# Mixture-of-experts stage of a two-block transformer: expert slots taken in pairs as 512-column products, token picking and spreading in split fp32r

## The reference, cut to what matters

```python
def swiglu(x, w_gu, w_down):
    g, u = jnp.split(x @ w_gu, 2, axis=-1)
    return (jax.nn.silu(g) * u) @ w_down

def moe_ffn(x, router, w_gu, w_down):
    xt = x.reshape(B * S, D)                     # 256 x 1024
    logits = (xt @ router).astype(jnp.float32)
    top_v, top_i = lax.top_k(logits, TOP_K)      # 2 of 8
    w = jax.nn.softmax(top_v, axis=-1)
    combine = jnp.einsum('tk,tke->te', w, jax.nn.one_hot(top_i, N_EXPERTS))
    y = jnp.zeros_like(xt)
    for e in range(N_EXPERTS):
        y = y + combine[:, e:e + 1] * swiglu(xt, w_gu[e], w_down[e])
    return y.reshape(B, S, D)
```

## Time and profile before

| | us |
|---|---|
| median of 3 runs | 2509.06 (2503.76 to 2511.31) |
| the profiled execution, whole | 2510.95 |
| its span, first to last instruction | 2509.0 |
| expert loop in it, 1452.72 to 2481.69 | 1029 |

### The profile page before, as it was taken

One profiled execution on the slowest core, in us unless ns is written; L12 is line 12 of the kernel. 1 busy time (PEld: TensorE's weight loads), 2 busy tenths in 40 slices (PEclk: granted clock), 3 DMA queues, 4 the chain that ended last, 5 costly groups with the idle time before them and its releaser, 6 DMA issues.

```text
span 2509.0 us, 43797 instructions
## 1 busy us (share of the span) xinstructions
PE 2419.1 (96%) x18302; PEld 2308.8 (92%) x18302; DVE 1887.7 (75%) x2272; ACT 1359.5 (54%) x1532; POOL 2.4 (0%) x8
## 2 busy tenths in 40 slices
PE   7799999999999999999998899999999999999998
PEld 6689999999999999899996799999999999999997
DVE  6666596888565969654566588888888888888886
ACT  4446333454444333433426367777676667676765
POOL 0000000000000000000000000000000000000000
PEclk9999999999999999999999999999999999999999
DMA  5124344532333455355331179988999999888995
GB/s 224 72 101 142 126 180 176 192 135 101 122 144 130 169 184 185 147 184 185 136 121 39 68 264 357 345 341 341 340 343 338 343 342 340 340 343 339 345 340 217
DMA packets 77279, 557.23 MB, mean 222 GB/s; under 512 B 8608, under 2 KB 8736, under 8 KB 10144
## 3 DMA queue, kind: packets, MB, share of 16 engines
q1 hardware_dynamic: 75888, 547.45, 58.7%
q10 hardware_dynamic: 1008, 6.49, 0.7%
q0 software_dynamic: 192, 0.52, 0.1%
HBM read 552.86 MB, written 1.05 MB: 221 GB/s over the span
## 4 chain that ended last, share of the span: by engine, by line
PE 90%; ACT 4%; DVE 4%; issue 2%; DMA 1%; SPq 0%; DVEq 0%; ACTq 0%
PE ps L890 13%; PE ps L892 13%; PE ps L891 13%; PE ps L1451 12%; PE ps L1453 12%; PE ps L1452 12%; PE ps L970 2%; PE ps L1001 2%; PE ps L1491 1%; PE ps L1445 1%; ACT whi L510 1%; PE ps L897 1%; PE ps L1248 1%; PE ps L1111 1%; PE ps L1079 1%
## 5 line engine op out<-in xcount | busy, mean ns | idle before, releaser
L1577 DVE TENSOR_TENSOR wlo<-raw,whi 128x2048 fp32r<-128x2048 f32 x519 | 1185.9, 2290 | 316.7 <-ACT whi L510 259.4
L510 ACT ACTIVATE whi<-raw 128x2048 fp32r<-128x2048 f32 x519 | 993.8, 1915 | 528.7 <-PE ps L892 375.1
L890 PE MATMUL ps<-hh,whi 128*128 128x256 f32 x2080 | 596.7, 287 | 9.6 <-DVE hl L1645 7.1
L891 PE MATMUL ps<-hl,whi 128*128 128x256 f32 x2080 | 591.7, 284 | 0.0
L892 PE MATMUL ps<-hh,wlo 128*128 128x256 f32 x2080 | 591.6, 284 | 0.0
L1451 PE MATMUL ps<-whi,hh 128*128 128x256 f32 x1792 | 523.3, 292 | 3.6 <-DVE work L2263 3.6
L1453 PE MATMUL ps<-wlo,hh 128*128 128x256 f32 x1792 | 507.9, 283 | 0.0
L1452 PE MATMUL ps<-whi,hl 128*128 128x256 f32 x1792 | 507.6, 283 | 0.0
L890 PEld LDWEIGHTS ps<-hh,whi 128*128 128x128 f32 x2080 | 402.7, 194 | 12.3 <-DVE hl L1645 8.5
L891 PEld LDWEIGHTS ps<-hl,whi 128*128 128x128 f32 x2080 | 402.7, 194 | 0.3
L892 PEld LDWEIGHTS ps<-hh,wlo 128*128 128x128 f32 x2080 | 402.4, 193 | 0.0
(11 more groups left out here) (332 smaller groups left out, 2771.0 us busy)
## 6 DMA issues: line engine op xcount, KB each, us to landing
raw<-stream SPq DMA_DIRECT2D x519, 1024.0 KB, 4.9
work<-w_in ACTq DMA_DIRECT2D x1, 2240.0 KB, 8.6
stage<-stage_consts ACTq DMA_DIRECT2D x4, 512.0 KB, 4.7
work<-mem_in ACTq DMA_DIRECT2D x2, 1024.0 KB, 4.9
x<-x_in SPq DMA_DIRECT2D x1, 1024.0 KB, 4.8
out<-x SPq DMA_DIRECT2D x4, 256.0 KB, 2.3
const<-consts SPq DMA_DIRECT2D x1, 548.5 KB, 5.8
work<-work POOLq DMA_DIRECT2D x4, 128.0 KB, 2.6
```

The lines of the kernel that those rows point to most:

```text
L510: nc.scalar.activation(whi[hi_at(g, odd)][:, :], raw[g % RAWS][:, :], ACT.Copy).then_inc(hi_ready, 1)
L890: mm(out_ap, hi_w, hi_x, start=start, stop=False, **kw)
L891: mm(out_ap, hi_w, lo_x, start=False, stop=False, **kw)
L1577: V.tensor_tensor(wlo[g % RAWS][:, :], raw[g % RAWS][:, :], whi[hi_at(g, odd)][:, :].bitcast(F32), ALU.subtract).then_inc(lo_ready[g % RAW ...
```

## The change

Only the expert stage changes.

1. **Gate/up slots in pairs.** SP no longer loads gate/up slots as they lie: it loads for an even slot of a pair the first half of the input blocks of both slots, for the odd one the second half. A piece that lies together in HBM is then 2 KB, not 8 KB, and a transfer has four for each partition. A pair thus accumulates in one whole PSUM bank over its two slots: per slot 4 x 3 matmuls of 512 columns. silu, multiply, turn and both keeps now come once for a pair, 256 columns wide (the turn is two 128-column ones). VectorE's and ScalarE's keeps of a pair now stand two pairs later, in even slots, behind the split of that slot; the turn stands behind the odd slot of the next pair.
2. **Gather** in two fp32r halves of the tokens (the 0/1 matrix is exact) for two experts at once, 256 columns, in two rounds (behind down slots 1 and 3 of an odd expert's second half) that use the same two banks; VectorE keeps each round (`keep_gathered`, behind its split of down slots 2 and 4).
3. **Spread** in fp32r: the 0/1 matrix unweighted, and the result, scaled by the slot's weight while it is kept, in a high part (ScalarE) and a low part (VectorE, `few_keep_y_lo`).
4. Before the loop: one more VectorE subtraction (2048 columns), no weighted matrices, two stretches of 14 matmuls on zeros; the turns of the 0/1 matrices move into expert 0's slots 2 and 6, with 16 one-column products.
5. The other branch (an expert with over 128 tokens) is rewritten to the new slot layout; it isn't run.

```diff
+            with sp.Fori(0, EXPERTS) as e:
+                for g in range(FIRST, FIRST + PER_EXPERT):
+                    sp.wait_ge(slot_used, e * PER_EXPERT + (g + 1 - RAWS))
+                    at, half = expert_slot(g)
...
+                        two = stream[bass.ds(e * PER_EXPERT + at, 2)].rearrange("two p (b h x) -> p b two h x", b=2, h=2)
+                        sp.dma_start(to[:, :].rearrange("p (b two x) -> p b two x", b=2, two=2), two[:, :, :, half]).then_inc(
...
 ScalarE, gate/up slots
+                        if s % 2:
+                            act.wait_ge(slot_used, e * PER_EXPERT + (gu.g + s + 1))
+                            act.wait_ge(few_tok, e * HALF + (q + 1))
+                            nc.scalar.activation(few_gate(q), ps[:, q % 2, 0:2 * P], ACT.Silu).then_inc(gate_act, 1)
-                        if s:
-                            few_keep_hi(e, j - 1)
                         split_hi(gu.g + s + DEPTH, e, e % 2)
+                        if s % 2 == 0 and s >= 4:
+                            few_keep_hi(e, q - 2)
...
 TensorE
+                for c in range(NB // 2):
+                    n = e % 2 * NB + s % 2 * 4 + c
+                    at = slice(n * P, (n + 1) * P)
+                    last = split_x(ps[:, bank, :].rearrange("p (m n) -> p m n", m=4), hh[:, at], hl[:, at], by_in(whi[hi_at(g, e % 2)], c),
+                                   by_in(wlo[g % RAWS], c), start=(s % 2 == 0 and c == 0), stop=(s % 2 == 1 and c == NB // 2 - 1))
...
+            def few_turn(e, q):
+                pe.wait_ge(few_tok, e * HALF + (q + 3))
+                pe.wait_ge(act_ready, e * HALF + (PHASES["moe_gu0"].a + q))
+                for n in range(2):
+                    last = turn(ps[:, 7, n * P:(n + 1) * P], few_tok_act(q)[:, n * P:(n + 1) * P])
...
+                        if s % 2 == 1 and q % (HALF // 2):
+                            few_turn(e, q - 1)
...
+                        if part == 1 and e % 2 and e < EXPERTS - 1 and s in (1, 3):
+                            if s == 1:
                                 pe.wait_ge(y_added, e * 2 + 1)
+                            else:
+                                pe.wait_ge(gather_kept, e + 2)
+                            few_gather((e + 1) // 2, s // 2, 5)
...
 VectorE
-                            if s:
-                                few_keep_lo(e, j - 1)
+                            q = part * (HALF // 2) + s // 2
+                            if s % 2:
+                                dve.wait_ge(gate_act, e * HALF + (PHASES["moe_gu0"].a + q + 1))
+                                V.tensor_tensor(few_tok_act(q), few_gate(q), ps[:, q % 2, 2 * P:4 * P], ALU.mult).then_inc(few_tok, 1)
                             split_lo(gu.g + s + DEPTH, e, e % 2)
+                            if s % 2 == 0 and s >= 4:
+                                few_keep_lo(e, q - 2)
+                            if part == 0 and s == 3 and e:
+                                few_keep_y_lo(e - 1)
                         for s in range(down.n):
                             split_lo(down.g + s + DEPTH, e, e % 2)
+                            if s in (0, 2):
+                                few_keep_lo(e, q - 1 + s // 2)
+                            if part == 0 and e and s in (3, 6):
+                                add_y(e - 1, s // 6)
+                            if part == 1 and e % 2 and e < EXPERTS - 1 and s in (2, 4):
+                                keep_gathered((e + 1) // 2, s // 4)
```

More of the change, by code:

```diff
@@ L147, in build @@
         mask_r = over("mask_r", "stage", 512, F32R)
+        few_r = over("few_r", "work", 12288, F32R)
         ident_r = over("ident_r", "const", P, F32R)
@@ L1430, in _ @@
             last.then_inc(x_turned, 1)
+            keep_warm(7, 14)
             pe.wait_ge(picked, 1)
@@ L1439, in _, with few_gather, few_give, few_slot_weights @@
             last.then_inc(counts_ps, 1)
-            def few_gather(e):
-                for c in range(NB):
+            keep_warm(7, 14)
+            def few_gather(pair, r, bank):
+                takes = few_r[:, FEW_TAKE + pair * 512:FEW_TAKE + (pair + 1) * 512].rearrange("p (e t n) -> p t e n", e=2, t=2)
+                for c in range(4):
+                    n = 4 * r + c
+                    to = ps[:, bank + c // 2, (c % 2) * 256:(c % 2 + 1) * 256].rearrange("p (e n) -> p e n", e=2)
+                    for part, tokens in enumerate((FEW_TOK_HI, FEW_TOK_LO)):
+                        for tt in range(2):
+                            last = mm(to, tokens[:, tt * 1024 + n * P:tt * 1024 + (n + 1) * P], takes[:, tt],
+                                      start=part == 0 and tt == 0, stop=part == 1 and tt == 1)
+                last.then_inc(gathered_ps, 1)
+            def few_give(half):
+                pe.wait_ge(places_built, 2)
+                for n in range(8):
+                    last = turn(ps[:, 5 + n // 4, (n % 4) * P:(n % 4 + 1) * P], few_take(4 * half + n // 2, n % 2).bitcast(F32))
+                last.then_inc(spread_ps, 1)
+            def few_slot_weights():
+                for e in range(EXPERTS):
                     for tt in range(2):
-                        take = bass.ds(e * 256 + (FEW_TAKE + tt * P), P)
-                        last = mm(ps[:, 5 + c // 4, (c % 4) * P:(c % 4 + 1) * P], FEW_TOK[:, tt * 1024 + c * P:tt * 1024 + (c + 1) * P],
-                                  work[:, take], start=(tt == 0), stop=(tt == 1))
-                last.then_inc(gathered_ps, 1)
+                        last = mm(ps[:, 2, e:e + 1], few_take(e, tt).bitcast(F32), small[:, 576 + tt * 8 + e:577 + tt * 8 + e],
+                                  start=e == 0 and tt == 0, stop=tt == 1, skip_group_check=True)
+                last.then_inc(slot_weights_ps, 1)
             def split_x(out_ap, hi_x, lo_x, hi_w, lo_w, start, stop, **kw):
@@ new lines, in keep_gathered @@
+                def keep_gathered(pair, r):
+                    dve.wait_ge(gathered_ps, 2 * pair + r + 1)
+                    kept = [keep_x_hi(r, odd, 5) for odd in range(2)]
+                    for odd in range(2):
+                        lo = keep_x_lo(r, odd, 5, kept[odd])
+                        if r:
+                            lo.then_inc(gathered, 1)
+                    V.memset(small[:, 639:640], 0.0).then_inc(gather_kept, 1)
+                V.memset(small[:, 638:639], 0.0).then_inc(few_tok, 2)
@@ new lines, in _ @@
+                for odd in range(2):
+                    if odd == 0:
+                        dve.wait_ge(gathered_ps, 1)
+                    first = keep_x_hi(0, odd, 5)
+                    if odd == 0:
+                        dve.wait_ge(gathered_ps, 2)
+                    second = keep_x_hi(1, odd, 3)
+                    keep_x_lo(0, odd, 5, first)
+                    keep_x_lo(1, odd, 3, second).then_inc(gathered, 1)
+                V.memset(small[:, 639:640], 0.0).then_inc(gather_kept, 2)
```

242 lines of the change are left out of this document (137 added, 105 removed).

## The result

The changed kernel takes **2810.97 us** (2802.43 to 2816.16, 4 runs) beside 2510.18 us before (2503.76 to 2512.97, 4 runs): ratio 1.1199, 95% interval 1.1159 to 1.1239. That is 301 us, 12.0% slower. The forecast was 2678, its range ended at 2740; 133 us are missing, and they are the subject of what follows. The profiled execution, from which all rows here come, took 2815.7 us, 4.7 above the median.

What follows compares the result with a forecast made beforehand. TensorE's own order, its instructions and its waits for VectorE, was taken to bound the loop. Experts of 145.6 to 156.9 us sum to 1201 against 1029, +172; 2509.1 + 172 - 3.4 = 2678 us, range 2650 to 2740.

Steps and rivals of the forecast that it cites:

- The waits: Expert loop: turns 1 to 6 of each half wait 2.16 us for VectorE's low keep, 96 times, 207 us.
- the 4.88: Microseconds from an even slot's end until VectorE's splits and keep are done and the turn can start; TensorE needs only 2.72.
- Rival (3): TensorE's clock falls in the turn waits: +70 us (2748) in a quarter of the pairs, +280 in all; chance 0.08.
- The rest of the ring: Loop: turn, even slot, ScalarE's split, VectorE's split, keep, next turn, repeating every 7.8 us for each waiting pair.
- rival 2: Weight loads in 2 KB pieces become the bound: +3 to +15 us at 336 GB/s, 2748 at 290; chance 0.07.
- The work: Pure TensorE work of an expert without a gather: 119.1 us, some 8 less than before; 512-column matmuls 0.227 apart.
- rival (4): Gate/up slots: four-piece 512-column operands run slower, +0.1 us a slot giving 2690; chance included in the forecast's 0.78.
- The start of expert 0: 16 turns and 16 one-column products in expert 0, at 0.12 and 0.04 us, 2.6 in all; expert 0 takes 145.6.
- The gather: Experts 1, 3, 5: second round waits 4.8 us, next expert's first slot some 1.7; with 4.0 of gathering 10.7 each.
- The ends: Outside the expert loop: it starts near 1449.3, 3.4 us earlier than before; behind the loop no change.
- Rival (1): The keep is not late, so no turn waits: loop 987 us, kernel 2464, faster than before; chance 0.05.

Runs made afterwards that it cites:

- the filling: Changed kernel with 8 matmuls on zeros ahead of each waiting turn, except in expert 0's first half: 2725.32 us, ratio 1.0852 (2722.52 in an earlier single run).
- kernel 1: Changed kernel with ScalarE's and VectorE's keeps of a pair moved into the next pair's odd slot, ahead of that slot's split: 2484.11 us, ratio 0.9899.
- two edits of order later: Changed kernel with the pair keeps, then also VectorE's keeping of the gather, moved ahead of the splits: 2457.70 us, ratio 0.9793.

## Why the prediction was wrong, step by step

- **The waits** (96 at 2.16, 207 us): right in place, count and size: 96, 212.8 us. The first one behind the down slots was up to 5.9 where I had 3.2 at most. (The three terms of the 4.88 add up to 4.90, 2 us in all.)
- **The clock** was the step that failed: the sum had no term for it. It took every slot at 0.227 because the loop of before has 1.00, and I left to a rival, since its wait was 2.49 and mine 2.16. The loop of before has hardly a wait; its clock tells nothing of a loop with 96. Rival (3) was the case, and had 0.08. It was mis-sized too: 10.5 to 10.7 us for a pair at the lower clock, "the keep then is in time"; measured 9.6, since only 3.4 us of the even slot ran slowly, and the keep was as late as ever, because that slot's end sets off the split. And it came in 50 of 96 pairs, between the quarter and the whole that I had priced, and ahead of 11 of 16 down slots, of which I had thought for none. Measured by the filling: **86 us**, and 5 more in expert 0's first half, which wasn't filled (two distances of 9.6 for 8.0, and 26.4 us for 24.8 from its last turn to the next half's first).
- **The rest of the ring**: in a waiting pair at full clock it is 8.00, not 7.80. In the rows above the keep starts at 1730.27 and the turn at 1730.83, 0.56, where the sum had 0.48; from an even slot's end to the turn it is 4.98 for 4.88, and the restart costs another 0.1 (the first matmul behind the turn has 0.31 for 0.227). **19 us.**
- **The 2 KB pieces** (rival 2, "+3 to +15" in the forecast): 13.5 us, but in the ring and not by a lower rate; 0 where nothing waits.
- **The work**: right. 0.227 for four-piece operands (1725.40 to 1725.62), so nothing for rival (4); an expert at 120.4 for 119.3; joining worth 28 of 35.
- **The start of expert 0**: from the loop's first matmul to the first turn 18.7 us, where my prices give 12.5 (4 slots 10.9, 8 turns 1.0, 16 one-column products at 0.04, 0.6). No row of before had such a product, and the 0.04 had no source. In the changed kernel:

```profile
1462.31 3.63 PE L1507 MATMUL ps<-small,few_r 128*128 128x1 f32 x32
...
1465.80 0.63 PE L1513 MATMUL ps<-whi,hh 128*128 128x512 f32 x1
```

```profile
1466.00:1469.40 3.40, 3.40 (x9) 2.63 (x9) 0.20 (x1) 0.15 (x1) 0.00 (x0) 0.50 0.24 92
```

  They take 3.5 us, two records for each, and the clock falls behind them for 3.4 us; it was low for 3.4 us at the loop's start, too, behind a wait of 2.0. In the kernels with 8 zeros and in kernel 1 the 18.7 are 18.4 to 18.5: **6 us** everywhere.
- **The gather**: waits of 4.4 us three times, where I had 4.8, and 1.0 ahead of the next expert for 1.7. Each was followed by 3.4 us at the lower clock (1780.0 to 1783.4, and two more), 1.6 us lost each time, which I hadn't. That is 3.3 us less and 4.9 more; the two nearly cancel, by luck.
- **The ends**: loop start 1451.55 for 1449.3 and the end of the loop to the end of the span 28.4 for 27.3: 3 us.
- **The sum of it**: 86 + 5 + 19 + 13.5 + 6 + 3 = 132.5 of 133. That it comes out so well is in part chance: the 86 and the 13.5 are differences of medians and carry some us each.
- **Rival (1)**, all keeps in time, 2464: two edits of order later the kernel stands at 2457.7.

The mechanism of the waits was right and gave the sign. What failed was the clock behind them, put at nothing in the sum and at 0.08 among the rivals, though the only row on idle TensorE, spoke of it. With it at half of the pairs and at the 1.6 us measured here, 48 x 1.6 = 77, the sum would have been 2755.

What stays open: why the clock falls behind one wait of 2.1 us and not behind the next. Among the pairs that stand behind a wait, slow and full clock mostly take turns: 49 of 64 neighbours differ, 15 are both slow, none are both at full clock. No run tells what decides it. The Trainium skill (TensorE: Matmul & The Clock Gate, A second HAM failure mode: psum-queue depth-cycling) tells of a kernel whose short idle times between groups of matmuls make the clock go back and forth between its levels; the rows here agree, and put 1.6 us on each fall.

## What to carry to other kernels

Before pricing a wait, draw the ring that repeats it and see whether TensorE's own work is in it: if it is, every loss there (clock, restart, a late block) comes on top, if not, the wait absorbs it. A short instruction that TensorE waits for belongs ahead of a long one on its engine, even when its own input allows both places: a keep of 0.4 us on VectorE, put two splits later with its like on ScalarE, cost 327 us. Where such a wait can't be avoided, a few matmuls on zeros ahead of it are a cheap way to learn what part of its price is the clock.

## What the runs showed of the hardware

- TensorE's clock fell behind waits of 2.1 us (a few up to 5.9) that came every 8 to 10 us, in 61 of 96 cases, mostly 0.3 to 1.5 us after work had started again, and for 3.4 us; with 1.15 us of idleness in their place it held in all of 79 cases (turns 8.0 apart).
- Matmuls on zeros count as work for it: 8 of them, 1.11 us, in 90 of the waits gave back 86 us.
- 16 one-column fp32 products took 3.5 us, 0.22 each, and TensorE's clock fell behind them for 3.4 us, though the records show no idle time of TensorE there.
- Loads in 2 KB pieces ran at 371 GB/s with a busy share of 1.02 of the DMA engines, the same rate as 8 KB pieces in the earlier trace rows at 0.97. The difference was in the waits for single blocks: 60.6 us in 72 places against 10.8 in 11 (kernel with 8 zeros).
- Joining two fp32r matmuls of 256 columns into one of 512, each with its weights loaded, saved 10.5 ns by the time of the whole kernel.
